# Later input tiles loaded and normalised after the first half's groups, in a three-layer float32 model on one core

## The chip, the core and the metric

The kernel runs on one core of one Trainium2 chip. The time is that of one execution on the device, in microseconds (us). The kernel before takes 3257.72 us, the median of 3 runs (3254.94 to 3258.13).

## The reference, cut to what matters

The model has two modulated blocks and then a block of mixers. Only the entrance of the first block bears on this change: the tokens `x` (1024 x 1024) and the context `ctx` (256 x 1024) are normalised row by row, modulated, and multiplied by `w_in`.

```python
def layer_norm(x):
    mu = jnp.mean(x, axis=-1, keepdims=True)
    var = jnp.mean(jnp.square(x - mu), axis=-1, keepdims=True)
    return (x - mu) * lax.rsqrt(var + LN_EPS)

def modulate(h, shift, scale):
    return layer_norm(h) * (1.0 + scale) + shift

# first_block, layer i = 0
sh1, sc1, g1, sh2, sc2, g2 = split(silu(c) @ ada_w[0] + ada_b[0], 6)
u  = modulate(x, sh1, sc1)
mc = split(silu(c_ctx) @ ada_w[0] + ada_b[0], 6)
uc = modulate(ctx, mc[0], mc[1])
p  = u @ w_in[0]                 # columns: conv 1536, q 512, k 512, v 512
kvc = uc @ w_in[0][:, K0:]       # the context gives keys and values only
...
```

Everything after this (attention over 1280 keys, output products, the MLPs, the Fourier block, the last block) follows from `p` and `kvc` and isn't touched.

## The kernel before, in words

Each engine has a program of its own, written out by hand; engines wait for each other on semaphores, and an engine does its instructions in the order written. Products with weights use three passes of matmuls (high x high, high x low, low x high; `three_passes`, L628 to L630): ScalarE writes the high part of an operand (`act_hi`, L634), VectorE the rest (`dve_lo`, L639).

**The entrance.** The 1024 tokens are 8 tiles of 128 tokens (TT = 8), in two halves of four (TPC = 4); the context is two more tiles, called 8 and 9 (CTT = 2). `act_start` loads tiles 0 to 2 from ScalarE's DMA queue, then `hat(t)` runs for all ten tiles. For a tile, VectorE takes the statistics (`dve_measure`, L778 and L781), ScalarE the square root (L792), VectorE the reciprocal and the bias (L798, L802), ScalarE writes the normalised tile (L881) and then issues the load of tile t + 3 (L874).

Meanwhile SyncE's queue brings 16 pages of the modulation weights `ada_w` (512 KB each: part 1, the scales, then part 0, the shifts) through three page buffers (L620). A page is free once TensorE has multiplied it with the conditioning columns (`pe_start`, L824). The same three buffers then take `w_in`: the pages of groups q0 to q3 and k0, and after them a mixture. So the first `w_in` page is issued when page 5 of part 0 has been used (`ada_taken (0, 0, 5)`, and 5 is KT - 3). Between the pages of part 0 TensorE transposes the first half's normalised tiles (L949).

**The projections.** `pe_project` does q0, q1, q2 on half 0, then transposes half 1 (L949, eight groups i, each of which needs tiles 4 to 7), does q3 on half 0, q0 on half 1, then transposes the context (`CTX_AT = (1, 1)`: ahead of q1 on half 1; L1008; it waits for tiles 8 and 9), and then q1 to q3 on half 1, the keys, the values and the convolution.

ScalarE's order is: high parts of the weights of groups 0 and 1 (the last lines of `act_start`), chunk 0 (`act_turn_chunk`: for each of 8 groups it modulates a transposed block, L959, and writes the high part, L634), weights 2 and 3, then for each group `rope` (it copies the result out of PSUM to a stage, L1097); at (3, 0) chunk 1 and weights 4. Chunk 1 begins when all eight transposes are done. VectorE goes in the same order: low parts of chunk and weights, rope (L1153 to L1158, four instructions), and after the weights some multiply-adds on further modulation pages (`dve_ada`, L695, L698). Three temporaries stand between ScalarE's L959 and VectorE's L639; ScalarE takes one again only when VectorE has read it. PSUM's eight banks are handed out as a ring: of half 1's transposes, groups 5, 6 and 7 take the banks that q0, q1 and q2 held.

GpSimd loads two tables for rope (512 KB each, L1221 and L1222) once the shifts are transposed (`ada_summed (0, 0)`), and stores the results of rope.

Of the kernel before, what the change touches and what calls it, by code (L numbers as in the profile page):

```python
# [8 lines left out]
P = 128  # L9
# [3 lines left out]
ACT = mybir.ActivationFunctionType  # L13
# [3 lines left out]
D = 1024  # L17
TT = T // P
KT = D // P
CH = 512  # L20
NCH = T // CH
TPC = CH // P
CTX = 256
CTT = CTX // P
# [764 lines left out]
def act_root(k, act, on, rows, *key):  # L789
    s = k.small[0:rows, k.smalls.of(*key), :]  # L790
    on.wait_ge(*k.measured.at(*key))
    act.activation(s[:, 14:15], s[:, 13:14], ACT.Sqrt, bias=k.eps[0:rows, 0:1]).then_inc(*k.rooted.inc(*key))  # L792
# [13 lines left out]
def scale_bias(k, rows, rms, *key):  # L806
    s = k.small[0:rows, k.smalls.of(*key), :]
    return s[:, 15:16], (k.eps[0:rows, 2:3] if rms else s[:, 14:15])
# [52 lines left out]
def token_tile(k, t):  # L861
    if t < TT:
        return k.H[:, t, :], k.XH[t // TPC][:, t % TPC, :], k.h_dma[t]
    return k.ctx_raw[:, t - TT, :], k.XHc[:, t - TT, :], k.ctx_in[t - TT]


def act_start(k, act, on):
    x = k.a["x"][0].rearrange("(t p) d -> p t d", p=P)
    ctx = k.a["ctx"][0].rearrange("(t p) d -> p t d", p=P)

    def load(t):
        if t < TT + CTT:
            dst, _, landed = token_tile(k, t)
            act.dma_start(dst, x[:, t, :] if t < TT else ctx[:, t - TT, :]).then_inc(*landed.inc("in"))  # L874

    def hat(t):
        src, dst, _ = token_tile(k, t)
        act_root(k, act, on, P, "x", t)
        scale, bias = scale_bias(k, P, False, "x", t)
        on.wait_ge(*k.scaled.at("x", t))  # L880
        act.activation(dst, src, ACT.Identity, bias=bias, scale=scale).then_inc(*k.hat_ok.inc("x", t))  # L881
        load(t + 3)

    on.wait_ge(*k.consts_ok.at())
    for t in range(3):
        load(t)
    on.wait_ge(*k.cols_ok.at(2))
    act.activation(k.cc[:, :, 0], k.columns("c", 0, 8), ACT.Silu)
    act.activation(k.cc[:, :, 1], k.columns("c_ctx", 0, 8), ACT.Silu).then_inc(*k.cc_ok.inc())
    on.wait_ge(*k.lam_ok.at("sums"))  # L890
    act.activation(k.lam[:, 2:4], k.lam[:, 0:2], ACT.Exp).then_inc(*k.act_done.inc("lam"))
    for t in range(TT + CTT):
        hat(t)
    for s in range(2):
        act_weights(k, act, on, s)


def dve_start(k, dve, on):
    dve.memset(k.ones[:], 1.0)
    for i, v in enumerate((1e-6, 1e-5, 0.0)):  # L900
        m = dve.memset(k.eps[:, i:i + 1], v)
    m.then_inc(*k.consts_ok.inc())
    at = 0
    for g, used in enumerate(k.col_groups):
        on.wait_ge(*k.vec_turned.at(g))
        dve.tensor_copy(k.cols[:, at:at + used], k.bank("vec", g)[:, 0:used]).then_inc(*k.cols_ok.inc(g))
        at += used
    lq = k.temp[4]
    on.wait_ge(*k.lambda_in.at())
    v = lq[:, 0:256].rearrange("p (a b d) -> p a b d", a=2, b=2)  # L910
    pairs = lq[:, 256:384].rearrange("p (a d) -> p a d", a=2)
    dve.tensor_tensor(pairs, v[:, :, 0, :], v[:, :, 1, :], ALU.mult).then_inc(*k.step.inc())
    on.wait_ge(*k.step.now())
    dve.tensor_reduce(k.lam[:, 0:2], pairs, AX_X, ALU.add).then_inc(*k.lam_ok.inc("sums"))
    on.wait_ge(*k.act_done.at("lam"))
    dve.tensor_tensor(k.lam[:, 4:5], k.lam[:, 3:4], k.lam[:, 2:3], ALU.subtract).then_inc(*k.step.inc())
    on.wait_ge(*k.step.now())
    dve.tensor_scalar(k.lam[:, 4:5], k.lam[:, 4:5], -LAM_INIT, None, ALU.add).then_inc(*k.lam_ok.inc())

    def hat(t):  # L920
        src, _, landed = token_tile(k, t)
        on.wait_ge(*landed.at("in"))
        dve_measure(k, dve, on, src, P, D, False, "x", t)
        dve_scale(k, dve, on, P, False, "x", t)

    def mod(part):
        on.wait_ge(*k.ada_taken.at(0, part, KT - 1))
        for half in range(2):
            dve.tensor_copy(k.ada_rows[0:2, part, half * CH:(half + 1) * CH],
                            k.bank("ada row", part, half)[0:2, :]).then_inc(*k.ada_row_ok.inc(part, half))  # L930

    for t in range(TT + CTT):
        hat(t)
        if t == TT - 1:
            mod(1)
    dve_mod(k, dve, on, 0, 1, 2)
    mod(0)
    dve_mod(k, dve, on, 0, 0, 2)
    for s in range(2):
        dve_weights(k, dve, on, s)  # L940
# [138 lines left out]
def act_project(k, act, on):  # L1079
    on.wait_ge(*k.mod_ok.at(0, 0))  # L1080
    scale, shift = (lambda i: k.mod[:, 0, 8 + i:9 + i]), (lambda i: k.mod[:, 0, i:i + 1])
    nothing = lambda: None

    def context():
        on.wait_ge(*k.turned.at("ctx", KT // 2 - 1))
        for j in range(KT):
            t = k.act_temp.take(on, ("ctx", j), (k.lo, ("uc", j)))
            v = k.temp[t]
            act.activation(v[:, 0:CTX], k.bank("ctx", j // 2)[:, (j % 2) * CTX:(j % 2 + 1) * CTX], ACT.Identity,
                           bias=k.mod_ctx[:, j:j + 1], scale=k.mod_ctx[:, 8 + j:9 + j]).then_inc(*k.taken.inc("ctx", j))  # L1090
            on.wait_ge(*k.taken.at("ctx", j))
            act_hi(k, act, on, k.Uc_hi[:, j, :], v[:, 0:CTX], "uc", j)

    def rope(what, h, c):
        on.wait_ge(*k.up_done.at("project", (what, h), c))
        n = take_stage(k, on, what, h, c)
        act.activation(k.stage[n][:], k.bank("up", "project", (what, h), c), ACT.Copy,  # L1097
                       scale=QK ** -0.5 if what == "q" else 1.0).then_inc(*k.taken.inc("rope", what, h, c))

    for c in range(NCH):  # L1100
        for i in range(4):
            if (i, c) in ((0, 0), (3, 0)):
                act_turn_chunk(k, act, on, "project", int(i == 3), scale, shift, nothing)
                for s in (2, 3) if i == 0 else (4,):
                    act_weights(k, act, on, s)
            if (i, c) == CTX_AT:
                context()
            rope("q", i, c)
            if c == NCH - 1:
                act_weights(k, act, on, 5 + i)  # L1110
    for h in range(HEADS):
        for c in range(NCH):
            rope("k", h, c)
        on.wait_ge(*k.up_done.at("kc", h))
        n = take_stage(k, on, "kc", h)
        act.copy(k.stage[n][:, 0:CTX], k.bank("kc", h)[:, 0:CTX]).then_inc(*k.taken.inc("kc", h))
        act_weights(k, act, on, 9 + h)
    for t in range(TT + CTT):
        on.wait_ge(*k.up_done.at("v", t))
        n = take_stage(k, on, "v", t)  # L1120
        act.copy(k.stage[n][:], k.bank("v", t)).then_inc(*k.taken.inc("v", t))
    for s in range(13, 17):
        act_weights(k, act, on, s)
    for t in range(TT):
        on.wait_ge(*k.hat_ok.at("x", t))
    for i in range(4):
        for part in range(3):
            m = 3 * i + part
            if part == 0:
                for c in range(NCH):  # L1130
                    on.wait_ge(*k.up_done.at("project", ("conv", m), c))
                    if i:
                        on.wait_ge(*k.dve_done.at("conv", m - 2, c))
                    act.copy(k.conv_gc[:, c * CH:(c + 1) * CH], k.bank("up", "project", ("conv", m), c)).then_inc(
                        *k.taken.inc("conv", m, c))
            if m < 7:
                act_weights(k, act, on, k.first["conv"] + 5 + m)
            for key in ATT_IN_PROJECT.get(m, ()):
                act_att_unit(k, act, on, k.att[key])


def dve_project(k, dve, on):
# [17 lines left out]
    for c in range(NCH):  # L1160
        for i in range(4):
            if (i, c) in ((0, 0), (3, 0)):
                dve_turn_chunk(k, dve, on, "project", int(i == 3))
                for s in (2, 3) if i == 0 else (4,):
                    dve_weights(k, dve, on, s)
            if (i, c) == CTX_AT:
                for j in range(KT):
                    v = k.temp[k.act_temp.of("ctx", j)]
                    dve_lo(k, dve, on, k.Uc_lo[:, j, :], v[:, 0:CTX], k.Uc_hi[:, j, :], "uc", j)
            rope("q", i, c)  # L1170
            if c == NCH - 1:
                dve_weights(k, dve, on, 5 + i)
# [2386 lines left out]
```

## Time and profile before

| | us |
|---|---|
| median of 3 runs | 3257.72 |
| profiled execution, its own time | 3257.9 |
| profiled execution, span | 3256.1 |
| TensorE busy | 3124.4 (96%) |
| VectorE busy | 2093.2 (64%) |
| ScalarE busy | 1283.4 (39%) |
| DMA, mean rate over the span | 72 GB/s |

The span is from the first to the last instruction. The profile's page cuts it into 40 slices; these three lines show TensorE, the granted clock and the DMA engines in tenths, 9 being 90% or more:

```profile
PE   7999899999999999889999999998998999999997
...
PEclk9999999999999999999999999998999999999999
DMA  7426311302332332111111111111111111111121
```

The first slice (0 to 81 us) is the only one below 8 for TensorE, and there the DMA engines are at 7.

### The profile page before, as it was taken

How to read it: one execution, taken by the hardware profiler on the slowest of the kernel's cores; microseconds unless marked ns; L12 is line 12 of the kernel's file. 1: busy time of each engine (PE TensorE's matmuls, PEld its weight loads, DVE VectorE, ACT ScalarE, POOL GpSimd, SP SyncE). 2: the span in 40 equal slices, each digit the busy share in tenths (PEclk: the TensorE clock that was granted, in tenths of full speed). 3: DMA queues.
4: the chain of work that ended last, by engine and by line, in shares of the span. 5: the costliest groups of instructions: out<-in, count | busy, mean ns of one | idle time of the engine just before them, and what ended most of it. 6: DMA issues, size and time to landing. Idle time of an engine off the chain costs nothing.

```text
span 3256.1 us, 36534 instructions
## 1 busy us (share of the span) xinstructions
PE 3124.4 (96%) x14623; PEld 2579.5 (79%) x14623; DVE 2093.2 (64%) x2729; ACT 1283.4 (39%) x1869; POOL 914.5 (28%) x476
## 2 busy tenths in 40 slices
PE   7999899999999999889999999998998999999997
PEld 2888788778888888677788888886887788888886
DVE  4725498577777776676756556656797665555555
ACT  4411487363333333342633333325136533333332
POOL 0001234244444441403343443321001032222210
PEclk9999999999999999999999999998999999999999
DMA  7426311302332332111111111111111111111121
GB/s 232 147 102 194 94 51 51 111 33 97 104 104 94 101 103 78 35 41 38 39 52 52 52 52 52 52 52 53 39 60 59 46 51 51 51 51 52 51 64 52
DMA packets 190484, 235.74 MB, mean 72 GB/s; under 512 B 9671, under 2 KB 149562, under 8 KB 190314
## 3 DMA queue, kind: packets, MB, share of 16 engines
q1 hardware_dynamic: 173338, 172.90, 17.2%
q10 hardware_dynamic: 8352, 30.41, 2.6%
q0 software_dynamic: 8624, 30.09, 2.5%
q8 instruction: 116, 1.90, 0.2%
q14 instruction: 54, 0.44, 0.0%
HBM read 217.64 MB, written 15.73 MB: 72 GB/s over the span
## 4 chain that ended last, share of the span: by engine, by line
PE 80%; DVE 10%; ACT 6%; issue 2%; DMA 1%; POOL 1%; SPq 0%; DVEq 0%; ACTq 0%; POOLq 0%
PE psum L628 25%; PE psum L630 25%; PE psum L629 25%; DVE page_r L639 2%; PE psum L1341 2%; DVE small L778 1%; ACT temp L959 1%; ACT page_r L634 1%; DMA page<-in_ada_w_dram 1%; DVE H L1621 1%; DVE U_lo L639 1%; PE psum L1316 1%; ACT U_hi L634 1%; PE psum L1317 1%; PE psum L824 1%
## 5 line engine op out<-in xcount | busy, mean ns | idle before, releaser
L628 PE MATMUL psum<-U_hi,page_r 128*128 128x512 f32 x2108 | 834.5, 396 | 23.2 <-DVE page_r L639 11.2
L629 PE MATMUL psum<-U_lo,page_r 128*128 128x512 f32 x2108 | 827.8, 393 | 0.0
L630 PE MATMUL psum<-U_hi,page_r 128*128 128x512 f32 x2108 | 827.6, 393 | 0.0
L639 DVE TENSOR_TENSOR page_r<-page,page_r 128x1024 fp32r<-128x1024 f32 x232 | 328.5, 1421 | 356.3 <-ACT page_r L634 337.8
L628 PEld LDWEIGHTS psum<-U_hi,page_r 128*128 128x128 f32 x2108 | 400.3, 190 | 115.7 <-DVE page_r L639 16.3
L634 ACT CAST page_r<-page 128x1024 fp32r<-128x1024 f32 (+2 forms) x323 | 337.2, 1047 | 381.9 <-PE psum L630 96.9
L630 PEld LDWEIGHTS psum<-U_hi,page_r 128*128 128x128 f32 x2108 | 400.1, 190 | 84.8
L629 PEld LDWEIGHTS psum<-U_lo,page_r 128*128 128x128 f32 x2108 | 400.7, 190 | 81.8
L628 PE MATMUL psum<-page_r,act_page_r 128*128 128x512 f32 x1176 | 457.5, 389 | 0.0
L629 PE MATMUL psum<-page_r,act_page_r 128*128 128x512 f32 x1176 | 457.5, 389 | 0.0
L2352 ACT ACTIVATE temp<-psum 128x512 f32<-128x512 f32 x192 | 114.6, 597 | 852.5 <-PE psum L630 807.0
L2410 DVE TENSOR_TENSOR H<-H,psum 128x512 f32<-128x512 f32 x556 | 358.3, 680 | 99.2 <-PE psum L630 99.1
L630 PE MATMUL psum<-page_r,act_page_r 128*128 128x512 f32 x1008 | 392.1, 389 | 0.0
L2507 POOL TENSOR_TENSOR page_r<-page,page_r 128x1024 fp32r<-128x1024 f32 x84 | 251.8, 3019 | 457.4 <-ACT page_r L634 457.4
L639 DVE TENSOR_TENSOR act_page_r<-act_page,act_page_r 128x512 fp32r<-128x512 f32 (+1 forms) x168 | 259.6, 1545 | 158.9 <-ACT act_page_r L634 157.3
L629 PEld LDWEIGHTS psum<-page_r,act_page_r 128*128 128x128 f32 x1176 | 220.7, 188 | 46.0
L628 PEld LDWEIGHTS psum<-page_r,act_page_r 128*128 128x128 f32 x1176 | 220.7, 188 | 45.8
L630 PEld LDWEIGHTS psum<-page_r,act_page_r 128*128 128x128 f32 x1008 | 189.2, 188 | 39.2
L2490 POOL TENSOR_TENSOR page<-page,row_gate 128x1024 f32<-128x1024 f32 x56 | 145.5, 2613 | 245.7 <-DMA page<-in_mlp_w_dram 245.7
L628 PE MATMUL psum<-page_r,U_hi 128*128 128x512 f32 x448 | 177.3, 396 | 16.8 <-ACT temp L959 5.1
L630 PE MATMUL psum<-page_r,U_lo 128*128 128x512 f32 x448 | 175.3, 391 | 0.0
L629 PE MATMUL psum<-page_r,U_hi 128*128 128x512 f32 x448 | 175.1, 391 | 0.0
(341 smaller groups left out, 4349.6 us busy)
## 6 DMA issues: line engine op xcount, KB each, us to landing
page<-in_mlp_w_dram SPq DMA_DIRECT2D x128, 512.0 KB, 4.1
page<-in_ada_w_dram SPq DMA_DIRECT2D x48, 512.0 KB, 4.9
page<-in_w_in_dram SPq DMA_DIRECT2D x38, 512.0 KB, 4.0
page<-in_w_up_dram SPq DMA_DIRECT2D x32, 512.0 KB, 4.1
page<-in_w_down_dram SPq DMA_DIRECT2D x32, 512.0 KB, 4.3
ada_land<-in_ada_w_dram ACTq DMA_DIRECT2D x24, 512.0 KB, 4.4
sum_page<-in_ada_w_dram ACTq DMA_DIRECT2D x12, 512.0 KB, 5.7
act_page<-in_ada_w_dram ACTq DMA_DIRECT2D x12, 512.0 KB, 9.5
```

The lines of the kernel that those rows point to most:

```text
L628: pe.matmul(out, l_hi, r_hi, start=start, stop=False, skip_group_check=read_between)
L629: pe.matmul(out, l_hi, r_lo, start=False, stop=False, skip_group_check=read_between)
L630: return pe.matmul(out, l_lo, r_hi, start=False, stop=stop, skip_group_check=read_between)
L634: return act.copy(hi, src).then_inc(*k.hi.inc(*key))
L639: return dve.tensor_tensor(lo, src, hi.bitcast(F32), ALU.subtract).then_inc(*k.lo.inc(*key))
L778: m = dve.bn_stats(s[0:rows, 6 * i:6 * i + 6], src[:, i * CH:min(width, (i + 1) * CH)])
L824: m = pe.matmul(k.psum[0:2, banks[half], :], k.cc[:, i, :], u.raw[:, half * CH:(half + 1) * CH], start=i == 0, stop=i == KT - 1)
L1341: m = pe.matmul(out, k.PT[i % 2][:, j, :], k.V[h % 2][:, j * P:(j + 1) * P], start=j == 0, stop=j == KEYS // P - 1)
L2352: act.activation(k.temp[t][:], k.bank("up", stage, i, c), ACT.Relu).then_inc(*k.relu_done.inc(stage, i, c))
L2410: m = dve.tensor_tensor(h, h, acc, ALU.add)
L2490: pool.tensor_tensor(u.raw, u.raw, k.row_gate[:], ALU.mult).then_inc(*k.pool_gated.inc(u.s))
L2507: pool.tensor_tensor(weight_part(k, p, 1), weight_sum(k, p), weight_part(k, p, 0).bitcast(F32), ALU.subtract).then_inc(*k.pool_lo.inc("wei ...
```

## The change

Four edits to `act_start`, `dve_start`, `act_project` and `dve_project`. Tiles 0 to 3 are loaded and normalised as before. Tiles 4 to 7 are loaded from ScalarE's queue when page 5 of part 0 has been used, ahead of weights 0 and 1; they are normalised on both engines after chunk 0 and weights 2 and 3, ahead of the first rope. Tiles 8 and 9 (the context) are loaded behind tiles 4 and 5 there, and normalised after chunk 1 and weights 4.

```diff
-def act_start(k, act, on):
+def act_load(k, act, t):
     x = k.a["x"][0].rearrange("(t p) d -> p t d", p=P)
     ctx = k.a["ctx"][0].rearrange("(t p) d -> p t d", p=P)
-    def load(t): ...
-    def hat(t): ...
-        load(t + 3)
+    dst, _, landed = token_tile(k, t)
+    act.dma_start(dst, x[:, t, :] if t < TT else ctx[:, t - TT, :]).then_inc(*landed.inc("in"))
+
+def act_token_hat(k, act, on, t):
+    src, dst, _ = token_tile(k, t)
+    act_root(k, act, on, P, "x", t)
+    scale, bias = scale_bias(k, P, False, "x", t)
+    on.wait_ge(*k.scaled.at("x", t))
+    act.activation(dst, src, ACT.Identity, bias=bias, scale=scale).then_inc(*k.hat_ok.inc("x", t))
+
+def act_start(k, act, on):
...
-    for t in range(TT + CTT):
-        hat(t)
+    for t in range(TPC):
+        act_token_hat(k, act, on, t)
+        if t == 0:
+            act_load(k, act, TPC - 1)
+    on.wait_ge(*k.ada_taken.at(0, 0, KT - 3))
+    for t in range(TPC, TT):
+        act_load(k, act, t)
     for s in range(2):
         act_weights(k, act, on, s)
+
+def act_later_tokens(k, act, on, first, end):
+    for t in range(first, end):
+        act_token_hat(k, act, on, t)
+        if t < TPC + CTT:
+            act_load(k, act, t - TPC + TT)
+
+def dve_token_hat(k, dve, on, t):
+    src, _, landed = token_tile(k, t)
+    on.wait_ge(*landed.at("in"))
+    dve_measure(k, dve, on, src, P, D, False, "x", t)
+    dve_scale(k, dve, on, P, False, "x", t)
...
 # dve_start
-    for t in range(TT + CTT):
-        hat(t)
-        if t == TT - 1:
-            mod(1)
+    for t in range(TPC):
+        dve_token_hat(k, dve, on, t)
+    mod(1)
     dve_mod(k, dve, on, 0, 1, 2)
...
 # act_project
                 for s in (2, 3) if i == 0 else (4,):
                     act_weights(k, act, on, s)
+                act_later_tokens(k, act, on, *((TT, TT + CTT) if i else (TPC, TT)))
...
 # dve_project
                 for s in (2, 3) if i == 0 else (4,):
                     dve_weights(k, dve, on, s)
+                for t in range(TT, TT + CTT) if i else range(TPC, TT):
+                    dve_token_hat(k, dve, on, t)
```

TensorE's, GpSimd's and SyncE's programs are as before.

## Rows read from the trace of the kernel before

**Rows 1.** Windows: length; busy us of PE, PEld, DVE, ACT, POOL; clock, DMA share, GB/s.

```profile
86.00:98.00 12.00, 11.05 (x48) 8.86 (x49) 5.84 (x9) 11.74 (x18) 0.43 (x1) 1.00 0.06 23
98.00:110.00 12.00, 12.00 (x62) 10.15 (x61) 11.59 (x17) 4.36 (x9) 1.08 (x2) 1.00 0.60 198
352.00:359.00 7.00, 1.36 (x9) 1.30 (x10) 4.93 (x12) 0.62 (x1) 1.26 (x1) 0.74 0.69 187
359.00:366.00 7.00, 7.00 (x27) 5.72 (x26) 2.99 (x2) 3.38 (x4) 0.00 (x0) 0.77 0.43 97
1378.00:1384.00 6.00, 5.81 (x16) 4.66 (x17) 5.90 (x12) 1.64 (x3) 1.98 (x1) 0.60 0.01 3
```

**Rows 2.** SyncE's loads (L620) in three stretches: issues, and times from issue to landing.

```profile
L620 SPq DMA_DIRECT2D page<-in_ada_w_dram x6: 328/328/328, 15.2 to 29.2; - x6
...
DMA to landing us min/median/max: 7.0/7.6/7.8
...
L620 SPq DMA_DIRECT2D page<-in_ada_w_dram x7: 327/328/328, 33.8 to 47.8; - x7
...
DMA to landing us min/median/max: 3.6/4.6/4.9
...
L620 SPq DMA_DIRECT2D page<-in_w_in_dram x2: 368/368/368, 58.5 to 60.4; - x2
...
DMA to landing us min/median/max: 7.7/7.8/7.8
```

**Rows 3.** Chain of waits, in order of time: start, length, what.

```profile
52.96 4.98 DMA page<-in_w_in_dram
...
82.29 3.51 PE psum L949 x32
```

**Rows 4.** DMA queues: two rows of 60 to 61.5 us, then one of 56.5 to 58.

```profile
DMA packets 142, 0.52 MB, mean 347 GB/s; under 512 B 15, under 2 KB 15, under 8 KB 142
...
q0 software_dynamic: 142, 0.52, 94.3%
...
q1 hardware_dynamic: 766, 0.39, 92.9%
```

**Rows 5.** Timeline from 50 to 60 us: start, length, engine, what, idle before.

```profile
50.27 8.63 SPq L620 DMA_DIRECT2D page<-in_w_in_dram  x4
...
57.13 0.17 DVE L717 SCALAR_TENSOR_TENSOR mod<-psum,cols 128x8 f32<-128x8 f32 x1 [0.50 <-PE psum L848]
...
57.96 1.05 ACT L634 CAST page_r<-page 128x1024 fp32r<-128x1024 f32 x1 [1.39 <-DMA page<-in_w_in_dram]
```

**Rows 6.** Timeline: two tiles' statistics and the first of them normalised.

```profile
13.28 1.28 DVE L778 BATCH_NORM_STATS2 small<-H 128x6 f32<-128x512 f32 x2
...
15.49 1.27 DVE L778 BATCH_NORM_STATS2 small<-H 128x6 f32<-128x512 f32 x2
...
15.61 1.24 ACT L881 ACTIVATE XH<-H,small 128x1024 f32<-128x1024 f32 x1 [0.48 <-DVE small L802]
```

**Rows 7.** Timeline from the end of chunk 0 to chunk 1; last two, ropes in a row.

```profile
70.70 2.36 DVE L639 TENSOR_TENSOR page_r<-page,page_r 128x1024 fp32r<-128x1024 f32 x2 [0.32 <-ACT page_r L634]
...
85.88 0.78 ACT L959 ACTIVATE temp<-psum,mod 128x512 f32<-128x512 f32 x1 [2.95 <-PE psum L949]
...
87.34 0.69 DVE L639 TENSOR_TENSOR U_lo<-temp,U_hi 128x512 fp32r<-128x512 f32 x1 [1.74 <-ACT U_hi L634]
...
132.01 0.74 DVE L1153 STREAM_SHUFFLE temp<-stage 128x512 f32<-128x512 f32 x1
...
134.78 0.74 DVE L1153 STREAM_SHUFFLE temp<-stage 128x512 f32<-128x512 f32 x1
```

**Rows 8.** Timeline: last low part of chunk 1, context transposes, the next rope.

```profile
96.68 0.69 DVE L639 TENSOR_TENSOR U_lo<-temp,U_hi 128x512 fp32r<-128x512 f32 x1 [0.64 <-ACT U_hi L634]
...
98.23 1.91 PE L1008 MATMUL psum<-ident,XHc 128*128 128x128 f32 x16
...
100.92 0.73 DVE L1153 STREAM_SHUFFLE temp<-stage 128x512 f32<-128x512 f32 x1
```

More of the change, by code:

```diff
@@ L864, in token_tile @@
     return k.ctx_raw[:, t - TT, :], k.XHc[:, t - TT, :], k.ctx_in[t - TT]
-def act_start(k, act, on):
+def act_load(k, act, t):
     x = k.a["x"][0].rearrange("(t p) d -> p t d", p=P)
     ctx = k.a["ctx"][0].rearrange("(t p) d -> p t d", p=P)
[L871 to L881, printed above, removed]
-        load(t + 3)
+    dst, _, landed = token_tile(k, t)
[7 more added lines that the diff above has]
+def act_start(k, act, on):
     on.wait_ge(*k.consts_ok.at())
     for t in range(3):
-        load(t)
+        act_load(k, act, t)
     on.wait_ge(*k.cols_ok.at(2))
@@ L891, in act_start @@
     act.activation(k.lam[:, 2:4], k.lam[:, 0:2], ACT.Exp).then_inc(*k.act_done.inc("lam"))
-    for t in range(TT + CTT):
-        hat(t)
+    for t in range(TPC):
[4 more added lines that the diff above has]
+    for t in range(TPC, TT):
+        act_load(k, act, t)
     for s in range(2):
         act_weights(k, act, on, s)
+def act_later_tokens(k, act, on, first, end):
[8 more added lines that the diff above has]
+    dve_scale(k, dve, on, P, False, "x", t)
 def dve_start(k, dve, on):
@@ L918, in dve_start @@
     dve.tensor_scalar(k.lam[:, 4:5], k.lam[:, 4:5], -LAM_INIT, None, ALU.add).then_inc(*k.lam_ok.inc())
[L920 to L924, printed above, removed]
     def mod(part):
```

## The prediction

> **What bounds the kernel now.** TensorE is busy for 96% of the span, so the places to look for are those where it is not. The page's slices show one: the first. I read next the chain of waits and the timeline of the first 140 us, then windows. Until 58 us TensorE has only small products and waits for pages; the chain goes through the page loads, and its last piece there is the load of a `w_in` page, 4.98 us [rows 3]. Between 59 and 98 us the two chunks decide. From 98 us on TensorE has no gap: 12.00 us busy of 12 [rows 1], and none above 0.8 us until 352.9. So whatever this change does to the moment at which that dense work runs, the end moves by the same amount. The later gaps begin when that dense work is done, so I let none of them absorb a shift.
>
> **Part 1: six loads leave the first 40 us.** Six pages issued from 15.2 to 29.2 us beside token tiles took 7.6 us to land, seven issued from 33.8 to 47.8 mostly alone took 4.6 [rows 2]: 3.0 us less for a page. The ring has three buffers, so six pages are two rounds and the gain is 2 x 3.0 = 6.0 us, less some 0.4 us in which tile 3 still shares the first round: 5.6 us. Page 5 of part 0 is then used at 50.2 - 5.6 = 44.6 us (the first `w_in` page is issued then, 50.27 now [rows 5]), and the modulation is there at 57.3 - 5.6 = 51.7 us [rows 5].
>
> **Part 2: where they go.** Tiles 4 to 7 are issued at 44.6 us, together with the first `w_in` page. ScalarE does weights 0 and 1 before it begins chunk 0, so chunk 0 waits for the landing of q1's page, 57.96 us now [rows 5], whatever the modulation does. Alone, q1's page would be issued near 47.4 and land 4.98 us later [rows 3], at 52.4. But 2.1 MB of tiles are in front of it or beside it. The nearest rows: two `w_in` pages issued at 58.5 and 60.4 us, beside 1.05 MB of rope tables, took 7.8 us [rows 2], 2.8 us more than 4.98; and from 60 to 61.5 us the 16 engines moved only the tables' packets (142, 0.52 MB, so near 4 KB each), while in 56.5 to 58 us SyncE's queue alone had moved 766 packets of 0.5 KB [rows 4]. The small packets of `w_in` lost nearly everything to the large ones. Bounds: at best q1's page isn't held up and lands at 52.4 (chunk 0 starts 5.6 us earlier); at worst it pays 2.8 us for each 1.05 MB, 5.6 for the tiles and 2.8 for the rope tables (issued at 51.7), and lands at 60.8 (2.9 us later). Between them: q1 is issued 2.8 us after the tiles, so about 1.2 us of their 5.6 are over before it matters, and the rope tables come just at its end: 52.4 + 4.4 + 0.2 = 57.0. Chunk 0 starts 57.0 - 57.96, about 1.0 us earlier. **Term: -1.0 us** (-5.6 to +2.9).
>
> The Trainium skill has a rule on this ("DMA: Bandwidth & Descriptors", "Queues, rings and completion order"): each DMA engine takes its queues in turn, a packet from each. By that rule, and one record of the trace as one packet, 512 token records would let 512 of q0's 1024 small ones through, and q1's page would land about where I put it; the rows from 60 to 61.5 us, with none of the small packets, are harsher than the rule. Its section "Issuing engines are not separate DMA queues" says that loads from ScalarE's and SyncE's queues run on the same 16 engines; the trace agrees, and it speaks against hoping that the moved loads are free.
>
> **Part 3: tiles 4 to 7 behind chunk 0.** (Times from here as if chunk 0 started when it does now; the shift is added at the end.) VectorE ends the low parts of weights 2 and 3 at 73.06 [rows 7]. A tile takes 15.49 - 13.28 = 2.21 us in a row of tiles, and 16.85 - 13.28 = 3.57 us from its statistics to the end of its normalisation [rows 6]. Four of them: statistics at 73.1, 75.3, 77.5, 79.7; tile 7 normalised at 83.3. TensorE has q0, q1, q2 to do, which hide this until its half-1 transposes at 82.2 (3.51 us in the chain, ending at 85.8 [rows 3]). They now start at 83.35 and end near 87.0: +1.15 us.
>
> Behind the tiles stand three ropes, on both engines. ScalarE copies q0 out at 83.3, VectorE starts its rope at 83.9. Ropes in a row take 134.78 - 132.01 = 2.77 us, so three end at 92.1. The first low part of chunk 1, now at 87.34 [rows 7], comes at 92.1. ScalarE has three temporaries; it can go on with group 3 at 92.85, when VectorE has read the first. From there a group costs 1.33 us (the eight starts of L639 from 87.34 to 96.68 are seven steps of 1.33 [rows 7, 8]) and its low part starts 1.46 us after ScalarE's start (85.88 to 87.34 [rows 7]): groups 3 to 7 at 94.3, 95.65, 97.0, 98.3, 99.65. The last low part ends at 100.3 and not at 97.4 [rows 8]: +2.9 us, which holds the 1.15. TensorE has q3 to do meanwhile (5.5 us from 87.0), then follows the low parts and ends q0 of half 1 about 1.0 us behind the last, at 101.3 (98.3 now).
>
> **Part 4: tiles 8 and 9 ahead of the context's transposes.** In TensorE's order the context's transposes come next, at 98.23 now [rows 8], and they wait for tile 9. On VectorE stand, behind the last low part, the low part of weights 4 and two multiply-adds: its next instruction is 100.92 - 97.37 = 3.55 us behind [rows 8]. Then the statistics of tile 8, 2.21 us later those of tile 9, and 3.57 us to its normalisation [rows 6]: 3.55 + 2.21 + 3.57 = 9.3 us behind the last low part, where TensorE arrives 1.0 us behind it. Nothing of TensorE's lies between. It waits 8.3 us, until 109.65. Parts 3 and 4 together: 109.65 - 98.25 = **+11.4 us**. The bounds are narrow, as every duration has its row: +9.5 if the ropes or tiles close up, +12.5 if the waits between engines add 0.1 to 0.2 us at each of some ten hand-overs. The loads of tiles 8 and 9 are issued near 77 and 79 us and have 20 us to land. On VectorE the ropes and low parts after the context start some 6 to 10 us later than now, less than TensorE's 11.4, so they aren't late.
>
> **Part 5: the clock after the stall.** Now TensorE has a granted clock of 1.00 in 86 to 110 us. After its 5.64 us gap that ended at 358.5 the clock was 0.77 over 7 us and 0.74 over the 7 before [rows 1]: 3.2 us and about 0.5 us at the lower level, 1.2 GHz, with work, in which half the time is lost, 1.85 us. After a 10.4 us gap it was 0.60 over 6 us [rows 1], 4.8 us at that level, 2.4 us lost. An 8.3 us stall lies between: **+2.0 us** (0 if it stays up, 2.4 at most).
>
> The Trainium skill says so too ("TensorE: Matmul & The Clock Gate", "Part 1: The HAM clock gate"): an array that stands idle falls to 1.2 GHz and comes back to 2.4 once it works again. Without it the sum would be 2.0 us less.
>
> **The sum.** -1.0 + 11.4 + 2.0 = +12.4 us on the profiled execution's 3257.9 us: 3270.3, say 3270. The median of the runs, 3257.72, is 0.2 below the profiled one, which changes nothing. Bounds added up: -5.6 + 9.5 + 0 = +3.9 and 2.9 + 12.5 + 2.4 = +17.8.
>
> **The rivals.** A: the moved tiles don't hold `w_in` up, chunk 0 starts 5.6 us earlier; parts 3 to 5 stay: +7.8, 3266. For it: `w_in` pages share when packets have one size. Against: rows 4. B: they hold it up entirely, rope tables included: +16.3, 3274; for it, rows 2 and 4, against it that q0 and q1 are issued 2.8 us apart and part of the tiles is gone. C, not slower: VectorE reaches tiles 8 and 9 early enough that TensorE doesn't wait at the context, and the start's 5.6 us are kept: -5.6 + 2.9 = -2.7 us with the late chunk 1, -5.6 without, so 3252 to 3255. It decides at one point: the 9.3 us from the last low part to tile 9's end would have to fall to the 1.0 us that TensorE needs. Against it stands the order of VectorE's program and every row of part 4. D: the stall is there, but a later wait that doesn't depend on it takes back some 7 us, most of all the gap at 352.9 (5.6 us): +5, 3263. Against it: that gap's length hangs on a load issued when convolution groups end. E: the pages don't come sooner, since each is bound by its own ring: term 1 is 0, the tiles are issued at 50.2 and hold `w_in` up by 4.6: +18, 3276.
>
> **How the numbers follow.** A change of 0.2% (6.5 us) is about what a measurement can tell from none. Forecast 0.52, A 0.18, B 0.12, C 0.06, D 0.08, E 0.04. Slower by over 6.5 us: the forecast, B and E, nearly all of A (0.16): 0.84. Within: D, the rest of A (0.02) and most of C, whose two prices lie inside 6.5 us (0.04): 0.14. Faster: 0.02, what is left of C, for a start that gains more than I count. The range: the forecast's own is 3266 to 3274; with A, B and a part of D, 3262 to 3276.
>
> **What would show it.** After: the shift of q0's first matmuls near -1 us, with `w_in` pages that take 8 us and more to land beside the tiles (A: 5 us); the half-1 transposes waiting about 1 us for tile 7; the largest new row, a wait of 8 us of TensorE ahead of L1008 on L881; a granted clock below 1 behind it; and from 130 us on each event 12 us later than now. I am wrong if L1008 starts less than 5 us later than now.

## The result: slower by about 14 us, close to the forecast

The changed kernel takes 3271.32 us (median of 5 runs, 3268.57 to 3272.43); the kernel before took 3257.18 in 5 runs beside them (3253.68 to 3258.13). The ratio is 1.0045, 95% interval 1.003 to 1.006. The profiled execution's span is 3270.3 us (3256.1 before): +14.2 where the sum said +12.4.

The place of the loss shows in four windows, in the columns of [rows 1]. The first two rows are the start and chunk 1; the third is a stretch in which TensorE was busy for 0.88 of 9 us; in the fourth it works again at a clock of 0.57 of full, that is mostly at 1.2 GHz.

```profile
50.00:61.00 11.00, 0.75 (x7) 0.51 (x5) 1.25 (x2) 2.21 (x3) 0.66 (x2) 0.76 0.85 288
88.00:102.00 14.00, 11.90 (x51) 8.47 (x49) 10.71 (x19) 11.46 (x17) 1.64 (x3) 1.00 0.15 57
102.00:111.00 9.00, 0.88 (x3) 0.40 (x3) 6.74 (x13) 2.97 (x5) 0.00 (x0) 0.77 0.50 175
111.00:118.00 7.00, 6.71 (x26) 6.09 (x27) 6.10 (x11) 4.80 (x10) 1.08 (x2) 0.57 0.10 37
```

The waits from 50 to 118 us name both causes (engine and line that waited, and for what; total us, times, longest). The first row is ScalarE ahead of weights 0, waiting for a `w_in` page; the last, TensorE at the context's transposes, waiting for the normalised tile 9. Lines have moved: L959, L1008, L881 of before are now L970, L1019, L879.

```profile
ACT page_r L634 <- DMA page<-in_w_in_dram: 35.3, 2, 34.8
...
PE psum L1019 <- ACT XHc L879: 8.4, 1, 8.4
```

How late each step is, from the timelines (start, length, what, idle time before it), beside [rows 5], [rows 7] and [rows 8]: weights 1 begin at 59.83 and not 57.96; chunk 1's last low part at 101.17 and not 96.68; the transposes at 111.29 and not 98.23.

```profile
59.83 1.04 ACT L634 CAST page_r<-page 128x1024 fp32r<-128x1024 f32 x1 [0.55 <-DMA page<-in_w_in_dram]
...
93.66 1.89 DVE L639 TENSOR_TENSOR U_lo<-temp,U_hi 128x512 fp32r<-128x512 f32 x3
...
101.17 0.69 DVE L639 TENSOR_TENSOR U_lo<-temp,U_hi 128x512 fp32r<-128x512 f32 x1 [0.64 <-ACT U_hi L634]
...
105.40 1.28 DVE L778 BATCH_NORM_STATS2 small<-ctx_raw 128x6 f32<-128x512 f32 x2
...
109.94 1.24 ACT L879 ACTIVATE XHc<-ctx_raw,small 128x1024 f32<-128x1024 f32 x1 [0.48 <-DVE small L802]
...
111.29 3.65 PE L1019 MATMUL psum<-ident,XHc 128*128 128x128 f32 x16 [8.41 <-ACT XHc L879]
```

And the loads. The three `w_in` pages issued from 42.9 us took 13.9 to 15.3 us to land, against 4.98 alone [rows 3]; SyncE's third issue was itself held for 7.15 us.

```profile
L620 SPq DMA_DIRECT2D page<-in_w_in_dram x3: 373/378/7152, 42.9 to 47.6; - x3
...
DMA to landing us min/median/max: 13.9/15.0/15.3
```

While tiles (ScalarE's queue), then rope tables (GpSimd's) flowed, SyncE's queue got 9 to 15% of the engines' time: first 49 to 52 us, then 54 to 56 (packets, MB, share). In these rows q10, q0 and q1 are names of DMA queues (ScalarE's, GpSimd's, SyncE's), not of weight groups. In the first stretch SyncE's queue had about one packet (0.5 KB) for each of the tiles' (near 4 KB), 262 beside 287; in the second about one for two, 100 beside 191.

```profile
q10 hardware_dynamic: 287, 1.04, 87.2%
q1 hardware_dynamic: 262, 0.13, 14.9%
...
q0 software_dynamic: 191, 0.71, 91.6%
q1 hardware_dynamic: 100, 0.05, 9.5%
```

### The profile page after: what moved, and what is told of

It is laid out like the page before. It is cut to its first block, busy times and chain, and to the rows that moved or that the text cites. A ratio compares the mean times of both kernels' runs of the same rounds, so it can differ in the third digit from the quotient of the medians.

```text
span 3270.3 us, 36534 instructions
## 1 busy us (share of the span) xinstructions
PE 3123.7 (96%) x14623; PEld 2579.4 (79%) x14623; DVE 2087.4 (64%) x2729; ACT 1283.5 (39%) x1869; POOL 917.4 (28%) x476
## 4 chain that ended last, share of the span: by engine, by line
PE 78%; DVE 11%; ACT 6%; issue 3%; DMA 1%; POOL 1%; SPq 0%; DVEq 0%; ACTq 0%; POOLq 0%
PE psum L628 24%; PE psum L629 24%; PE psum L630 24%; DVE page_r L639 2%; PE psum L1355 2%; DVE small L778 2%; ACT page_r L634 1%; ACT temp L970 1%; DVE H L1635 1%; PE psum L1330 1%; DVE U_lo L639 1%; PE psum L824 1%; PE psum L1331 1%; ACT U_hi L634 1%; DMA page<-in_ada_w_dram 1%
## 5 line engine op out<-in xcount | busy, mean ns | idle before, releaser
L639 DVE TENSOR_TENSOR page_r<-page,page_r 128x1024 fp32r<-128x1024 f32 x232 | 318.6, 1378 | 369.2 <-ACT page_r L634 358.6
```

The lines of the kernel that those rows point to most:

```text
L639: return dve.tensor_tensor(lo, src, hi.bitcast(F32), ALU.subtract).then_inc(*k.lo.inc(*key))
```

## The experiments

All are edits of the changed kernel. Ratios are to the kernel before in the same session (3256.3 to 3256.8). The columns of moments come from one profiled execution of each kernel. "q1 ready" is ScalarE's start of weights 1; the moment at which page 5 is used varies by 1 to 2 us between executions, so the next column counts from the issue of q0's page, which happens then. "Dense work" below is TensorE's stretch without gaps, from the context's transposes on.

| | q0 issued | q1 ready | from issue | chunk 0 | wait at context | us, median | ratio to before (95%) |
|---|---|---|---|---|---|---|---|
| before | 50.3 | 57.96 | 7.7 | 58.92 | 0 | 3257.2 | |
| changed | 42.9 | 59.83 | 16.9 | 60.78 | 8.4 | 3271.3 | 1.0045 (1.003, 1.006) |
| e1 context later | 44.1 | 60.69 | 16.6 | 61.64 | 2.9 | 3265.5 | 1.0029 (1.0018, 1.0039) |
| e2 tiles behind w | 43.6 | 51.59 | 8.0 | 54.27 | 8.4 | 3266.7 | 1.0029 (1.0017, 1.004) |
| e3 rope tables late | 44.7 | 58.27 | 13.6 | 59.22 | 8.4 | 3269.7 | 1.0038 (1.0025, 1.0051) |
| e4 tiles in 1 KB | 44.9 | 55.5 | 10.6 | 56.43 | 8.4 | 3269.2 | 1.0037 (1.0023, 1.0052) |
| e5 both | 43.3 | 50.80 | 7.5 | 54.12 | 2.9 | 3257.6 | 1.0007 (0.9998, 1.0015) |
| e6 + rope behind | 43.4 | 50.45 | 7.0 | 52.89 | 5.1 | 3259.3 | 1.001 (1.0001, 1.0019) |
| e7 context in start | 47.8 | 55.11 | 7.3 | 58.45 | 0 | 3255.8 | 1.0001 (0.9992, 1.001) |
| e8 paced, 4 KB | 43.0 | 60.38 | 17.4 | 61.33 | 8.4 | 3272.9 | 1.0054 (1.0038, 1.0069) |
| e9b tiles on SyncE | 44.0 | 51.52 | 7.6 | 52.47 | 8.4 | 3264.0 | 1.0025 (1.0016, 1.0034) |
| e10b + tiles first | 42.8 | 50.60 | 7.8 | 51.55 | 0 | 3252.5 | 0.999 (0.9981, 0.9999) |
| e11b + rope behind | 43.9 | 52.48 | 8.6 | 53.44 | 0 | 3250.5 | 0.9982 (0.9973, 0.9991) |
| e12b e7 on SyncE | 45.3 | 52.75 | 7.5 | 53.70 | 0 | 3256.1 | 0.9998 (0.9989, 1.0007) |

**The stall at the context.**

```diff
-CTX_AT = (1, 1)
+CTX_AT = (2, 1)
```

> Edit: the context's transposes and its chunk stand ahead of q2 on half 1 and not ahead of q1; all else as in the changed kernel. My theory (TensorE's wait of 8.4 us for context tile 9, and the lower clock behind it, 2.8 us, are the largest part of the loss): TensorE does q1 on half 1 (5.5 us) inside the wait, 2.9 us of it stay, the clock stays up: 8.3 us less than the changed kernel, 3263. Rival (VectorE, busy 16 to 17 us of 20 in 100 to 140 us, is what bounds this stretch; the wait only moves): a new wait of TensorE at the context's keys (kc of head 0), under 4 us gained, 3268 or more.

The wait fell from 8.4 to 2.9 us as forecast, and no new one came. The gain is 5.8 us, not 8: in the profiled execution chunk 0 started 0.9 us later, and the clock fell even after 2.9 us of waiting. Windows behind the wait, of e1 and then of e5 with the same 2.9 us of waiting, show 0.74 against 1.00: the same short wait was followed by the lower clock in one profiled execution and not in the other, and why isn't shown.

```profile
112.00:118.00 6.00, 5.89 (x28) 5.44 (x29) 5.28 (x11) 2.41 (x5) 0.54 (x1) 0.74 0.11 44
```

```profile
105.00:111.00 6.00, 6.00 (x36) 5.19 (x34) 5.78 (x11) 1.91 (x3) 0.82 (x2) 1.00 0.13 46
```

**The pages of the start.** e2 moves the four loads behind the two waits of `act_weights`:

```diff
-    on.wait_ge(*k.ada_taken.at(0, 0, KT - 3))
-    for t in range(TPC, TT):
-        act_load(k, act, t)
     for s in range(2):
         act_weights(k, act, on, s)
+    for t in range(TPC, TT):
+        act_load(k, act, t)
```

> Edit: tiles 4 to 7 are loaded behind the high parts of weights 0 and 1, that is once both first w_in pages have landed, and not with them. My theory (the w_in pages of groups q0 and q1 were held up by the tiles and by the rope tables, their small packets losing to 4 KB ones): the pages land 5.0 to 5.5 us after their issue (12 to 15 us in the changed kernel), q1's at 51 us and not 59.8, chunk 0 starts at 52, 8.5 us earlier, and all that follows too: 3263. Rival 1 (the pages are held up by the rope tables alone): 3 us, 3268. Rival 2 (the tiles, issued now at 52, come too late, or hold up the pages of q2 and q3, so that weights 2 and 3 wait at the end of chunk 0): chunk 0 earlier, but the end of weights 3 not, 3270.

q1's page is ready 8.0 us after q0's issue and not 16.9, and dense work is 7.7 us earlier than in the changed kernel. Rival 1 falls, rival 2 too: nothing waits at the end of chunk 0. Chunk 0 starts 2.3 us later than I said. The page came 0.6 us later, and ScalarE then issues the four loads first (2.56 us from 51.60, of which 1.63 us, put down to "issue", stand idle ahead of chunk 0):

```profile
51.59 1.04 ACT L634 CAST page_r<-page 128x1024 fp32r<-128x1024 f32 x1 [0.69 <-DMA page<-in_w_in_dram]
51.60 2.56 ACTq L871 DMA_DIRECT2D H<-in_x_dram  x4
54.27 0.78 ACT L969 ACTIVATE temp<-psum,mod 128x512 f32<-128x512 f32 x1 [1.63 <-issue]
```

The median gained only 4.6 us, 3266.7 where I expected 3263. That is less than the 7.7 us of the trace; 2.0 us of the difference arose behind 130 us in the two profiled executions (see "After 130 us" below); the rest isn't explained.

e3 takes only the rope tables away from there:

```diff
 # pool_project
     on.wait_ge(*k.ada_summed.at(0, 0))
+    on.wait_ge(*k.lo.at("u", "project", 0, 3))
     pool.dma_start(k.rope_cos[:], k.a["rope_cos"])...
```

> Edit: the two rope tables (1.05 MB) are loaded once group 3 of chunk 0 is done, and not at the shifts; tiles as in the changed kernel. My theory (tiles and tables hold up w_in by about their own transfer time, 2.8 us for each 1.05 MB): q1's page lands near 57.0 and not 59.8, everything from chunk 0 on is 2.8 us earlier: 3268.5. Rival (only the tiles on ScalarE's queue matter, as the tables come after): no change, 3271.

From issue to ready 13.6 us, 3.3 less: their share. The rest of the excess over 7.5 us, 6.1, is that of the tiles. In the time it is 1.6 us where I expected 2.8 (the profiled execution used page 5 only at 44.7), which the intervals don't separate from none; the trace does.

e4 and e8 ask whether it is bytes, packets, or the moment of issue:

```diff
+    if TPC <= t < TT:
+        for j in range(4):
+            w = slice(j * (D // 4), (j + 1) * (D // 4))
+            act.dma_start(dst[:, w], x[:, t, w]).then_inc(...)
+        return
```

> Edit: each of tiles 4 to 7 is loaded in four column slices, so in packets of 1 KB and not 4 KB; same bytes, same place in ScalarE's queue (16 issues for 4, about 5.5 us of issuing on an idle ScalarE). Packet theory (the engines take a packet from each queue in turn, so a queue of 0.5 KB packets gets a ninth beside 4 KB ones and a third beside 1 KB ones): q0's page lands 3 us or more earlier than 58.2, q1's 2 to 4 us earlier than 59.8; 3268 to 3269. Rival (the bytes in front count, not the packets' size): q0 and q1 land as in the changed kernel, 58 to 60, 3271.

```diff
     on.wait_ge(*k.ada_taken.at(0, 0, KT - 3))
-    for t in range(TPC, TT):
-        act_load(k, act, t)
+    act_load(k, act, TPC)
+    on.wait_ge(*k.ada_taken.at(0, 0, KT - 2))
+    act_load(k, act, TPC + 1)
+    on.wait_ge(*k.ada_taken.at(0, 0, KT - 1))
+    act_load(k, act, TPC + 2)
+    on.wait_ge(*k.mod_ok.at(0, 0))
+    act_load(k, act, TPC + 3)
```

> As the changed kernel, with the loads of tiles 4 to 7 spaced: one each when pages 5, 6, 7 of part 0 have been used and one when the shifts are done, so over some 7 us, like the slices of e4_tiles_in_1kb (16 issues in 9.4 us), but in 4 KB packets. q1's w_in page landed 16.9 us after page 5 was used in the changed kernel and 10.6 us after it in e4. Packet theory: still 14 us or more. Rival (it was the spacing of the issues that helped e4, not the packets' size): 10 to 12 us.

10.6 us with 1 KB packets spread over 9.4 us, 17.4 us with 4 KB packets spread over 7.5. For q1's page the spacing alone gained next to nothing, as the packet theory said. But it isn't nothing elsewhere: q0's page landed 10.1 us after its issue in e8, 7.0 in e4 and 15.3 in the changed kernel, so spacing took 5 us off that page with the packets as large as ever. And in e8 the trace shows what kept q1's page. In the trace a load ends with sixteen counts on its semaphore, as many as there are DMA engines; I read each as one engine's. Of the sixteen that end q1's page, thirteen had come by 52.8 us (7.1 us after its issue; in e4 the thirteenth came after 7.5), the last two at 56.4 and 60.4. A page is ready when its last count has come. In the changed kernel the counts of q0's page run from 48.0 to 58.2 us, and the same page took 1.8 us between first and last count before. So both the size of the packets and the moment of the issues count. The two runs don't separate them cleanly: e4's slices also come later (1.35 MB of tiles had moved from 44 to 56 us, 1.95 in e8), and each is one profiled execution. The intervals of the two times overlap, too.

e9b puts the same loads into the queue of the pages, behind q2's page:

```diff
     k.landing(u).also(u.n)
+    if u.n == 2 * KT + 2:
+        for t in range(TPC, TT):
+            act_load(k, sp, t)
...
 # act_start
-    on.wait_ge(*k.ada_taken.at(0, 0, KT - 3))
-    for t in range(TPC, TT):
-        act_load(k, act, t)
```

> As the changed kernel, but tiles 4 to 7 are loaded from SyncE's queue, behind q2's w_in page, and not from ScalarE's. Theory (a load from another queue overtakes the w_in pages packet by packet, one behind them in their own queue doesn't): q0's and q1's pages land 5 us after their issue, near 48.5 and 51, and ScalarE has no loads to issue ahead of chunk 0 (4 issues took 2.6 to 3.2 us in e2, e5 and e7): chunk 0 starts at 52, about 2.5 us earlier than in e2_tiles_behind_w: 3264 (e2: 3266.7, changed kernel 3271). Rival (only the bytes in flight count): q1 lands at 57 to 60, 3270.

```profile
49.74 1.05 ACT L637 CAST page_r<-page 128x1024 fp32r<-128x1024 f32 x1 [28.03 <-DMA page<-in_w_in_dram]
51.52 1.04 ACT L637 CAST page_r<-page 128x1024 fp32r<-128x1024 f32 x1 [0.74 <-DMA page<-in_w_in_dram]
52.47 0.77 ACT L970 ACTIVATE temp<-psum,mod 128x512 f32<-128x512 f32 x1
```

7.6 us, as without any competitor (7.7 before), and chunk 0 directly behind weights 1; 3264.0 where I expected 3264. By itself this doesn't answer the rival (bytes in flight): behind q2's page the tiles are issued only from 49.1 to 52.0 us, 5 us and more after q0's page, when q0's and q1's are nearly there. What answers it is q2's page. It was issued at 48.7 us, 0.4 us ahead of the four tiles in the same queue, with the rope tables at 50.7, and landed in 6.0 us (5.0 in e2 without the tiles; 5.5 to 5.7 in e10b, e11b and e12b). The nearest comparison is q0's page in the changed kernel, issued together with the same four tiles from another queue: it took 15.3. The price is paid by the next page: q3's, issued behind the tiles, took 12.1 us, which nothing waits for.

**Do the gains add?** e5 is e1 and e2 together. e6 has in addition, in `dve_project`:

```diff
                 dve_turn_chunk(k, dve, on, "project", int(i == 3))
+                if i == 3:
+                    rope("q", 2, 0)
...
-            rope("q", i, c)
+            if (i, c) != (2, 0):
+                rope("q", i, c)
```

> Edits of e1_context_later and e2_tiles_behind_w together. If the two losses are separate (the start by the held-up pages, the stall by the tiles on VectorE), their gains add: chunk 0 starts 4.6 us earlier than in the kernel before, chunk 1 costs 2.6 more, the wait at the context is 2.9: +0.9 on the kernel before, 3258 (that kernel 3257). If VectorE's backlog were the bound (rival), the earlier start would only lengthen the wait at the context: 3262 or more.

> As e5_both, and VectorE does the rope of q2 on half 0 behind the low parts of chunk 1 and not ahead of them. Theory of part 3 (three ropes behind the four tiles hold up the first low part of chunk 1): the first low part comes 2.8 us earlier, then ScalarE sets the pace, the last low part comes 1.8 us earlier than in e5_both: 3256, level with the kernel before. Rival (the rope is only moved onto the way to the context's tiles): the wait at the context grows by the same 1.8 to 2.8, no gain on e5_both.

e5: 3257.6, the two losses are separate and nearly all of the 14 us. e6: 3259.3, no gain, and the rival was right. The wait at the context grew from 2.9 to 5.1 us, as the rope now stood between chunk 1 and tile 8; the first low part came earlier and tile 9 didn't.

e7 brings tiles 8 and 9 back into the start with e2's loads and e6's rope (shortened; tiles 8 and 9 also leave their later place on both engines):

```diff
 # act_start
-        if t == 0:
-            act_load(k, act, TPC - 1)
+        if t < 3:
+            act_load(k, act, (TPC - 1, TT, TT + 1)[t])
+    for t in range(TT, TT + CTT):
+        act_token_hat(k, act, on, t)
 # dve_start
-    for t in range(TPC):
+    for t in (*range(TPC), TT, TT + 1):
         dve_token_hat(k, dve, on, t)
```

> Tiles 8 and 9 are loaded and normalised in the start, behind tile 3, as the kernel before does in a later place; tiles 4 to 7 are loaded behind weights 0 and 1 (e2) and normalised behind chunk 0; rope of q2 behind chunk 1's low parts (e6); context's transposes where they were. Theory: no wait at the context at all; the start gives back about 2.0 us of its 4.6 for 1.05 MB more; chunk 1 costs 0.8: -1.8 us on the kernel before, 3255. Rival (the start's loads bind as before once two more tiles are in it): no gain in the start, 3258.

No wait at the context. Page 5 is used at 47.8 us here and 45.3 in e12b, 46.6 on average; with four tiles in the start it was 43.7 on average over eleven kernels (42.8 to 44.9): 2.9 us for 1.05 MB, not 2.0, though the two kernels differ by 2.5 us between themselves. Time: level with the kernel before, between theory and rival.

**A better version.** e10b is e9b with `CTX_AT = (2, 1)` and, at (3, 0) on both engines, the two context tiles ahead of weights 4 and their multiply-adds; e11b has in addition VectorE's rope of q2 behind those two tiles (VectorE's part, shortened):

```diff
 # dve_project, (i, c) == (3, 0), after dve_turn_chunk
+    for t in range(TT, TT + CTT):
+        dve_token_hat(k, dve, on, t)
+    rope("q", 2, 0)              # e11b only
     dve_weights(k, dve, on, 4)
-    for t in range(TT, TT + CTT):
-        dve_token_hat(k, dve, on, t)
```

> e9b, the context's transposes ahead of q2 on half 1 (e1), and tiles 8 and 9 normalised ahead of weights 4 and the two multiply-adds, not behind them. Theory: chunk 0 starts 7 us earlier than in the kernel before, chunk 1 costs 2.6, tile 9 is ready 5.9 us behind chunk 1's last low part, TensorE comes for it 6.5 us behind: no wait. TensorE's dense work runs 4.4 us earlier than before: 3252. Rival (VectorE's backlog moves the wait to the context's keys of head 0): a wait of 2 to 4 us there, 3255.

> e10b with VectorE's rope of q2 on half 0 behind chunk 1 and tiles 8 and 9 (in e6 it stood between chunk 1 and the tiles and gained nothing). Theory: the last low part of chunk 1 comes 1.8 us earlier and nothing else waits: 3250. Rival (VectorE's backlog): the context's keys wait by as much, 3252.

3252.5 and 3250.5, where 3252 and 3250 were expected. In e10b tile 9 is ready 5.7 us behind chunk 1's last low part and TensorE comes for it 6.3 us behind. e11b beats the kernel before by 0.18% (0.09 to 0.27), the changed one by 0.6%. Its windows, in the columns of [rows 1] and over the same stretches as those of the changed kernel above, hold no wait above 0.4 us and no fall of the clock:

```profile
88.00:102.00 14.00, 13.86 (x70) 11.39 (x69) 11.02 (x22) 8.91 (x14) 0.54 (x1) 1.00 0.06 19
102.00:111.00 9.00, 9.00 (x41) 7.46 (x40) 8.71 (x14) 1.55 (x2) 1.08 (x2) 1.00 0.73 241
111.00:118.00 7.00, 7.00 (x32) 5.82 (x31) 6.57 (x9) 3.67 (x7) 0.54 (x1) 1.00 0.82 277
```

Counted from chunk 0's start, dense work came 2.6 us later than before in e10b and 0.8 in e11b: the rope's 1.8 us. In the medians the two intervals overlap.

> e7 with tiles 4 to 7 loaded from SyncE's queue behind q2's w_in page. In e7 q1's page landed at 55.1 us and ScalarE then issued four loads for 3.2 us before chunk 0. Theory: those 3.2 us are gained, 3253. Rival (the loads cost nothing on the path, the modulation was what chunk 0 waited for): as e7, 3256.

Inconclusive. In the trace chunk 0 starts 4.75 us earlier than in e7 (2.5 of it from an earlier page 5, the rest ScalarE's issues), and dense work at 187 us is 4.4 us earlier; the medians, 3256.1 and 3255.8, show none of it. The profiled spans, 3254.0 and 3254.4, differ by 0.4 us only, as the later stretches gave the difference back: 2.9 us of it between 2200 and 2400 us, where e7 gained 3.0 us on the kernel before and e12b 0.1. What decides there, and in the medians, I didn't test.

## Why the prediction was right, and where it was off

**Direction, time and range** held: 3270 forecast, 3271.3 measured, 3262 to 3276 the range. The mechanisms held too; that the total came so close is in part luck, as the sum was 3.4 us low at 130 us (12.4 against 15.8) and the clock of a later stretch gave some of it back. The steps, on the profiled execution:

| step | predicted | measured |
|---|---|---|
| page 5 of part 0 used | 5.6 earlier | 7.4 earlier (42.9) |
| chunk 0's start (the term of part 2) | -1.0 (-5.6 to +2.9) | +1.9 |
| chunk 1 behind tiles 4 to 7 | +2.9 | +2.6 |
| parts 3 and 4 together | +11.4 | +11.2 (13.06 less 1.87) |
| wait at the context | 8.3 | 8.41 |
| clock behind it | +2.0 | +2.8 |
| whole shift, from 130 us on | +12.4, unchanged | +15.8, at the end +14.2 |

**Part 1** was undersized: with the later tiles gone, the pages gained 7.4 us and not 5.6 (6.6 on average over the eleven kernels): eight pages issued from 14.4 to 29.1 us now took 4.4 us to land (median), 7.6 before. Its gain reached nobody, as part 2 swallowed it. It hid the size of part 2's error, though: 16.9 us from a page 5 at the forecast 44.6 would have put weights 1 at 61.5, 3.5 us late, past the worst bound of +2.9.

**Part 2 is the term that was mis-sized.** The mechanism was right, and the sign of the term wrong: +1.9 us and not -1.0. I let q1's page land between the two, 12.4 us after page 5 was used, and it landed like rival B, behind both rope tables and 16.9 us after (my worst bound was 16.2). I had counted transfer time (2.8 us for each 1.05 MB), and took off what would be over before q1 was issued. What the runs show is that a page doesn't wait for the mean of the engines: sixteen counts finish it, and the last came 10 us behind the first. The rule of the Trainium skill that I cited beside the sum ("DMA: Bandwidth & Descriptors", "Queues, rings and completion order": a packet from each queue in turn) fits the stretch from 49 to 52 us, 262 small packets beside 287 large ones, if a record of the trace is taken as the packet of the rule; the page itself lets a packet be several descriptors, and no run here tells which it is. It doesn't fit 54 to 56 us (100 beside 191 of the rope tables) or the 142 beside none of [rows 4]. e4 agrees with it, as the pages lost far less beside 1 KB packets, but e4 against e8 isn't a clean test. Taken over all engines together it is too mild for a landing: from 45 to 53 us some 1,200 small packets had run, more than the 1,024 of q0's page, and the page was not ready before 58.2.

**Parts 3 and 4** held to 0.3 us, since each duration had a row and the order of each engine is written in the kernel. e1 and e5 confirm the cause by taking most of it away; e6 that what stands between chunk 1 and tile 9 is on the path, whichever work it is; e10b that no wait is left when weights 4 and the multiply-adds go behind the tiles (9.3 us become 5.7) and TensorE does q1 first.

**Part 5.** The 16 transposes took 3.65 us and not 1.91 [rows 8], and the window behind stood at 0.57: 0.43 x 7 x 2 = 6.0 us at the lower level with work in them, 3.0 lost, 2.8 in the timeline. I had interpolated between 1.85 and 2.4; the stretch at the lower level after the stall was simply longer.

**After 130 us.** The shift was 15.8 us through the projections, 17.4 before 2300 us, 14.2 from 2350. The last step is the granted clock of a stretch in which both kernels do the same work: the windows show it, first before, then after.

```profile
2290.00:2345.00 55.00, 55.00 (x265) 46.72 (x266) 45.50 (x66) 9.39 (x15) 0.00 (x0) 0.88 0.14 39
```

```profile
2306.00:2359.00 53.00, 53.00 (x279) 45.54 (x278) 45.30 (x66) 9.49 (x16) 0.00 (x0) 0.94 0.14 40
```

0.12 x 55 less 0.06 x 53 is 3.4 us. It isn't particular to this change: between 2200 and 2400 us ten of the thirteen edited kernels gained 2.3 to 4.0 us on the one profiled execution of the kernel before, and e2, e6 and e12b 0.1 at most. A single profiled span is worth no more than that. The rival that a later gap absorbs the delay (D) is out: the gap ends at 374.3 us and is 5.59 us long, 5.64 before.

**The reading of the slices.** Both the section on the time before and the prediction call the first slice the only one in which TensorE is below 8. The last slice is at 7 as well. It has no part in the sum, since its work comes after everything that was changed and shifts as a whole (14.2 us at 3200 us as at 2400).

## What to carry to other kernels

When work is moved from a place where engines idle to one where an engine's order is fixed, follow each engine in order from the moved work to the next thing TensorE waits for: here 9.3 us of VectorE's list against 1.0 us of TensorE's gave a wait of 8.4 us, over half of the 15.8, and the 2.8 that the clock cost came behind it; putting both lists in order of who is waited for made the wait nothing. When a load is moved, look at what it will meet: large packets from a second queue held small ones up by more than their own transfer time (10.1 us for 3.15 MB that by the rows would take 8.4), and a load put behind them in their own queue cost the page ahead of it 1 us. A gain at the start counts only if the thing that was really waited for (a page, here, not the modulation) comes sooner.

## What was not expected of the hardware

- One page's sixteen counts spread over 10.2 us (48.0 to 58.2) beside 4 KB traffic from another queue; the same page's spread over 1.8 us before, and over 1.8 to 3.7 us in the kernels whose tiles were issued later.
- Issuing isn't free when earlier transfers are in flight: four loads took ScalarE 2.3 to 3.2 us to issue in e2, e5, e6 and e7 (1.4 to 2.3 us of it ahead of chunk 0), and SyncE's single issue of q2's page took 7.15 us, where 0.33 to 0.38 is usual.
- A wait of 2.9 us was followed by a clock of 0.74 in one kernel (e1) and 1.00 in another (e5).
